# Rounded input tiles that all begin at one place of a 128-byte frame, or at eight

## What is computed

```python
h = rmsnorm(x, norm_mix_g); proj = h @ w_in          # 44 slabs of 128 output columns
merged = g_a * (y_a @ w_branch_hg) + g_b * (y_b @ w_branch_conv)
x = x + merged @ w_out
x = x + peer_ffn(rmsnorm(x, norm_ffn_g), ...)         # 128 x 128 single-neuron experts
for layer in range(2):                                # second block
    x = x + 0.5 * swiglu(rmsnorm_2(x), gate, up, down)    # D_FF = 2816
    x = x + (even_mixer, odd_mixer)[layer](rmsnorm_2(x))
    x = x + 0.5 * swiglu(rmsnorm_2(x), gate2, up2, down2)
return rmsnorm_2(x, norm_final)
```

## Time and profile before

| | |
|---|---|
| median of 3 runs | 2041.58 us (2041.24 to 2041.86) |
| span of the profiled execution | 2039.6 us |
| PE (matmuls) busy | 2005.6 us, 98% of the span, 13232 matmuls |
| PEld (LDWEIGHTS) busy | 1822.9 us, 89%, as many |
| DVE (VectorE) busy | 1508.3 us, 74% |
| ACT (ScalarE) busy | 1123.1 us, 55% |
| DMA | 353.73 MB, mean 173 GB/s |
| granted TensorE clock | 9 tenths or more in all 40 slices of the span |

### The profile page before, as it was taken

How to read it: one execution, slowest core, us unless ns; L and a number is a source line. 1 busy time by engine, 2 the same in 40 slices (tenths; PEclk the granted TensorE clock), 3 DMA queues, 4 the chain that set the end, 5 groups by cost and what they waited for, 6 DMA issues and landing times.

```text
span 2039.6 us, 37233 instructions
## 1 busy us (share of the span) xinstructions
PE 2005.6 (98%) x13232; PEld 1822.9 (89%) x13232; DVE 1508.3 (74%) x2564; ACT 1123.1 (55%) x1835; POOL 59.9 (3%) x40
## 2 busy tenths in 40 slices
PE   7999999999999999999999999999999999999998
PEld 6999999988888888888888999999999999999998
DVE  5868898877777777777777667776667667957666
ACT  5445537965555555555555555755555555655554
POOL 0000430000000000000000000000000000000000
PEclk9999999999999999999999999999999999999999
DMA  6445543055565666655665555455555555445553
GB/s 214 135 135 190 205 142 104 24 174 187 189 192 192 187 189 192 191 189 187 206 231 173 187 186 174 135 169 188 187 186 178 185 185 186 156 143 177 185 188 111
DMA packets 101466, 353.73 MB, mean 173 GB/s; under 512 B 11392, under 2 KB 16640, under 8 KB 101120
## 3 DMA queue, kind: packets, MB, share of 16 engines
q1 hardware_dynamic: 100944, 350.13, 52.5%
q10 hardware_dynamic: 432, 2.36, 0.3%
HBM read 348.77 MB, written 3.67 MB: 173 GB/s over the span
## 4 chain that ended last, share of the span: by engine, by line
PE 90%; DVE 7%; ACT 2%; issue 1%; DMA 0%; SPq 0%; DVEq 0%; ACTq 0%
PE front L2030 38%; PE acc L2030 35%; PE tile L2030 16%; DVE w_lo L1219 2%; ACT w_hi L715 1%; DVE rstd L1241 1%; ACT h_parts L741 0%; DMA raw<-stream 0%; PE front L2587 0%; DVE cand L1688 0%; DVE h_parts L1248 0%; DVE sq L1230 0%; DVE conv L1573 0%; DVE rest L1657 0%; DVE top_i L1653 0%
## 5 line engine op out<-in xcount | busy, mean ns | idle before, releaser
L1219 DVE TENSOR_TENSOR w_lo<-raw,w_hi 128x1024 fp32r<-128x1024 f32 x612 | 747.0, 1223 | 85.4 <-ACT w_hi L715 84.9
L715 ACT CAST w_hi<-raw 128x1024 fp32r<-128x1024 f32 x628 | 654.3, 1044 | 137.6 <-PE tile L2030 60.8
L2030 PE MATMUL front<-h_parts,w_hi 128*128 128x512 f32 (+1 forms) x2432 | 586.4, 377 | 4.2 <-ACT h_parts L741 2.5
L2030 PEld LDWEIGHTS front<-h_parts,w_hi 128*128 128x128 f32 x2432 | 436.5, 189 | 80.2 <-issue 2.4
L2030 PE MATMUL front<-h_parts,w_lo 128*128 128x256 f32 x2272 | 337.2, 282 | 0.0
L2030 PEld LDWEIGHTS front<-h_parts,w_lo 128*128 128x128 f32 x2272 | 318.8, 190 | 20.6
L2030 PE MATMUL tile<-h_parts,w_hi 128*128 128x256 f32 x1344 | 247.8, 286 | 5.1 <-DVE w_lo L1219 2.6
L2030 PEld LDWEIGHTS tile<-h_parts,w_hi 128*128 128x128 f32 x1344 | 209.5, 192 | 8.2 <-issue 4.9
L1304 DVE TENSOR_TENSOR scaled<-front,scaled 128x512 f32<-128x512 f32 x76 | 52.6, 692 | 215.1 <-ACT scaled L779 215.1
L2030 PE MATMUL acc<-w_hi,mid_hi 128*128 128x512 f32 x512 | 200.9, 392 | 2.1 <-DVE mid_lo L1793 1.7
L783 ACT ACTIVATE scaled<-scaled 128x256 f32<-128x256 f32 x188 | 78.6, 418 | 223.4 <-DVE scaled L1307 116.6
(11 more groups left out here) (324 smaller groups left out, 2519.5 us busy)
## 6 DMA issues: line engine op xcount, KB each, us to landing
raw<-stream SPq DMA_DIRECT2D x632, 512.0 KB, 3.7
early_u<-stream SPq DMA_DIRECT2D x20, 512.0 KB, 3.6
early_activations<-early_out SPq DMA_DIRECT2D x20, 128.0 KB, 3.5
scaled<-early_activations SPq DMA_DIRECT2D x10, 128.0 KB, 4.0
x<-x_t SPq DMA_DIRECT2D x2, 512.0 KB, 5.3
keysT<-keys_t ACTq DMA_DIRECT2D x1, 1024.0 KB, 6.3
attc<-attention_constants ACTq DMA_DIRECT2D x1, 1024.0 KB, 7.1
out_t<-h SPq DMA_DIRECT2D x4, 256.0 KB, 2.4
```

Of the source, the lines that this page charges most:

```text
L715: nc.scalar.copy(w_hi[:, s, :], raw[:, s, :]).then_inc(hi_ready, 1)
L1219: nc.vector.tensor_tensor(w_lo[:, s, :], raw[:, s, :], w_hi[:, s, :].bitcast(F32), ALU.subtract).then_inc(lo_ready, 1)
L2030: return nc.tensor.matmul(out, lhsT, rhs, start=start, stop=stop, **kw)
```

## The change

The eight tiles of `h_hi` and of `h_lo` get 16 bytes of padding each (`LINE` = 4 elements), so that a tile is 1040 bytes behind the one before it: tile k begins at byte 16·k of a 128-byte frame, from 0 to 112, and its `h_lo` at the same byte as its `h_hi`. The two buffers of `mid_hi` begin at bytes 16 and 48 of a 64-byte frame, those of `mid_lo` at 32 and 0. What lies behind them in SBUF moves by 448 bytes, which is 64 in a 128-byte frame: `y_hi` and `y_lo` go from byte 32 of it to byte 96. `w_hi` and `w_lo` stay. No instruction is added, dropped or moved on any engine; in the first norm alone four copies of ScalarE and four subtractions of VectorE that wrote two tiles as 512 elements in one run now write them as two runs of 256.

```diff
+LINE = 4
+H_TILE = T + LINE
+MID_TILE = T + 2 * LINE
 H_HI = 3 * RING * D
-H_LO = H_HI + KT * T
-MID = H_LO + KT * T
-COLS = MID + 5 * 2 * T
+H_LO = H_HI + KT * H_TILE
+MID = H_LO + KT * H_TILE
+MID_HI = MID + 6 * T
+MID_LO = MID_HI + 2 * MID_TILE
+COLS = MID + 5 * 2 * T + 12 * LINE
...
-        h_parts = sb("h_parts", H_HI, [2, KT, T], F32R)
-        assert H_LO == H_HI + KT * T
+        h_padded = sb("h_parts", H_HI, [2, KT, H_TILE], F32R)
+        h_parts = h_padded[:, :, :, 0:T]
...
-        mid_hi = sb("mid_hi", MID + 6 * T, [2, T], F32R)
-        mid_lo = sb("mid_lo", MID + 8 * T, [2, T], F32R)
+        mid_hi = sb("mid_hi", MID_HI, [2, MID_TILE], F32R)[:, :, LINE:LINE + T]
+        mid_lo = sb("mid_lo", MID_LO, [2, MID_TILE], F32R)[:, :, 2 * LINE:2 * LINE + T]
```

## The result

The changed kernel takes 2048.35 us (median of 6 runs, 2048.11 to 2048.7) beside 2041.64 us for the kernel before in the same session: ratio 1.0033, 95% interval 1.0022 to 1.0045. It is slower by 6.7 us, where 16.9 us less was forecast. The time lies inside the range of 1995 to 2055 us, on the other side of no change; it is within 2 us of the rival named *Slower* (2047 us).

A forecast was written before the change was run, and what follows sets the result against it. PE, busy 98% of the span, was taken as the bound through its matmul intervals. Savings of 11.1 us (256 columns) and 5.8 us (512) sum to 16.9 us off 2041.6, about 2025 us; range for 8 in 10: 1995 to 2055 us.

The forecast's parts named there:

- Slower: 512-column matmuls never settle with a new starting byte every tile: 16.6 us lost against 11.1 won, 2047 us; chance 0.24.
- The bound and the reading: PE, busy 98% of the span, sets the end; matmul intervals must be read as distances between starts.
- The 13 ns surplus depends on the places: Matmul intervals exceed their columns by about 13 ns; operand starting places affect it, as y's 118.15 against 120.0 ns suggests.
- The first rival, no change: y projections are quicker for another reason than their byte, so moving operands does nothing: 2041.6 us; chance 0.18.
- Which matmuls get another place: Count of matmuls moved off byte 0 in h_parts and mid: 6016 of 256 columns, 3128 of 512.
- The term of 256 columns: Projections, fronts and SwiGLU drains: 6016 matmuls each save y's 1.85 ns, 11.1 us less.
- The term of 512 columns: Fronts and expert drains: 3128 matmuls each take the same 1.85 ns saving, 5.8 us less.
- Much more: All operands at byte 0 may be the worst case; half the bounded surplus goes, 2002 us; chance 0.13.

The follow-up runs named there:

- e1: Against the kernel before, only the h_parts tiles get their eight places, mid stays at byte 0: 2044.23 us, ratio 1.0014.
- e7: Against the kernel before, all of h_parts moved by 128 bytes and mid by 256: 2046.14 us, ratio 1.0023.
- e5: Against the kernel before, mid and what lies behind it moved by 128 bytes, h_parts unmoved: 2043.71 us, ratio 1.0013.
- e8: Against the kernel before, every tensor in SBUF, weights too, moved by 64 bytes, all distances kept: 2041.20 us, ratio 1.0.
- e3: Against the kernel before, all h_parts tiles at byte 32 without padding between them, mid moved by 128 bytes: 2044.85 us, ratio 1.0017.
- e4: Against the kernel before, all h_parts tiles at byte 64 of a 128-byte frame, mid moved by 128 bytes: 2040.03 us, ratio 0.9996.
- e6: Against the kernel before, all h_parts tiles at byte 64, mid moved by 256 bytes: 2041.11 us, ratio 1.0.
- e2: Against the kernel before, only mid_hi and mid_lo get their four places, h_parts stays at byte 0: 2044.04 us, ratio 1.0016.

## Why the prediction was wrong, step by step

*The bound and the reading.* Right. The end is set by the intervals of PE; the groups' sums give the whole difference of the spans, and the gaps over 160 ns in the projections grew by no more than 1.5 us.

*The 13 ns surplus depends on the places.* Right, and now shown without the `y` tiles: e1 and e7 move `h_parts` against the weights, e5 moves `mid`, and the intervals of those matmuls change that read it; e8 moves all and changes none. The first rival, no change, falls with it. The rule set against the change there, the Trainium skill's independent read ports (TensorE: Matmul & The Clock Gate, section Step-by-step: what each phase is for), does not hold in the sense that neither operand's place could matter to the other: the 512-column fronts took 483.7 us before and 492.7 in e1, with the same instructions. That the two streams of reads collide is still only argued: the runs show that the distance matters, not what happens in the memory. The plain float32 rows are weak support for it as well: the trace shows how often a record starts (216 ns), not how often it reads its operand.

*Which matmuls get another place.* Counted in a frame of 128 bytes, while by the runs 256 is what counts (moves by 128 matter in e5 and e7, one by 256 does not in e1). Within 256 `h_lo` of tile k stands at 128 + 16·k (it lies 8320 bytes behind `h_hi`), and both buffers of `mid_lo` are off zero. So every wide front and every drain got another place, 3648 matmuls of 512 columns and not 3128, and the `h_lo` matmul of tile 0 moved too, which fits its 118.6 ns.

*The term of 256 columns.* Forecast 11.1 us less, measured 2.4 + 3.0 + 3.1 + 1.1 = 9.6 us less. The value read from `y` at one place carried over to other places, to within a fifth in the sum; by group it was between 1.2 ns (fronts, 2.4 us / 1988) and 2.1 ns (projections, 119.9 to 117.8 ns without the gaps). There was some luck in it: not only bytes 16 and 48 were without a row, but 64 to 112 as well. The lower bound named there is not the shortest interval of the trace either (bf16 matmuls of 128 columns start 56 ns apart), but the sum does not use it.

*The term of 512 columns.* This is the step that failed: "each matmul, wide or not, has one LDWEIGHTS of 128 columns beside it and shows the same surplus of 13 ns, so I take the same saving for each". Forecast 5.8 us less, measured 9.0 + 6.6 = 15.6 us more, 15.6 us / 3128 = 5.0 ns for each matmul counted as moved. The same 13 ns were the best case tried of one width and the worst of the other. The rows said as much: 512 columns had never shown a shorter interval than the settled one, only longer, 230 to 240 ns behind a change of width. I took a row of the same type but of the other width, and left the rows of the same width to the rival.

*The rival Slower.* Its price (5.3 ns for each, 16.6 us) and its time (2047 us) are near what was measured (5.0 ns, 15.6 us, 2048.35 us). Its mechanism is right in half, so the price is in part luck: at equal places a 512-column stream settles at 227 ns and in the changed kernel it does not. But "a new starting byte at every tile" is not the reason. In e3 all tiles stand at one byte and the front shown takes 234 ns for each matmul all the same. And its point against itself, that the excess may be a buffer that fills, would have made the excess die out at any place, which it does not.

*Much more.* It did not come: the largest gain of a 256-column group in the table is that of the fronts in e4, 268.5 us against 274.1, and no run brought the 512-column groups visibly below 483.7 and 354.1.

*What stays open.* Why equal places settle at 227 ns and others not, why 128 bytes are not equal places while 256 are (e5 and e7 against e1 and e6), and which distance is best for 256 columns; of the distances tried there 32 bytes is among the best. How a rhythm is handed from one group to the next (e2, e6, e7), and why executions of one kernel differ by up to 4.6 us where the distance is not zero, was seen and not explained.

## What to carry to other kernels

When a matmul's interval is longer than its columns, read it for each width apart before moving anything: the same surplus in ns can be a good place for one width and a bad one for the other, and a row of another width is no price. Distances between moving and stationary operand are a parameter of a hand-made layout worth one run each; here equal places modulo 256 bytes for 512 columns and unequal ones for 256, given by two views of one room, brought 0.36%. And where the rows of before show a disturbance that only lengthens an interval, that lengthening is a price to set beside the hoped-for gain, even if its reason is not known: here it came within 0.3 ns, and its reason was another. A kernel whose runs spread more than those of before needs more than one trace for a difference of a few us.

## What the runs showed of the hardware that was not expected

- The interval of reduced-float32 matmuls depends on the distance between the two operands' addresses, and repeats closely: with all tensors moved by 64 bytes each group's sum stays within 0.2 us of before; with `h_parts` moved by 32 to 128 bytes (e1, e3, e4, e6, e7) the 512-column intervals of the fronts go from 483.7 us / 2112 = 229 ns on average to between 230 and 233.
- A move by 256 bytes leaves the intervals as they were, one by 128 does not (expert drains 353.9 us in e1, 358.2 in e5, 354.1 before).
- At equal places modulo 256 bytes the 512-column drains settle at 226.7 ns in every trace that has them: from the sixth of twelve matmuls on in the kernel before, the eighth in e6, the tenth in e7. In e4, with `mid` 128 bytes further, all twelve go back and forth between 229 and 238 ns. (These are averages for each of the twelve, over about a hundred drains of a trace.)
- 256-column matmuls can do better than the averages of the table: in e4 the eight of a SwiGLU front take 1110.73 - 1109.83 = 0.90 us, 113 ns each. In e6 the same distance gave 1106.25 - 1105.31 = 0.94 us, 118 ns; what decides between the two is open.
